# Selection rounds moved behind the value chunks, modulation sums spread, in a two-block fp32 kernel

## What is computed

```python
mod = (c_act @ w_ada[l] + b_ada[l])[:, None, :]
sh1, sc1, g1, sh2, sc2, g2 = jnp.split(mod, 6, axis=-1)
h = _rmsnorm(x, norm_g[l, 0]) * (1.0 + sc1) + sh1
y = _hybrid_mixer(h, ...)            # z = h @ w_in, mixers A, B, C, gates, w_out
x = x + g1 * _rmsnorm(y, norm_g[l, 1])

# mixer C, the sparse one: each query keeps 64 of up to 256 keys
score = jnp.einsum('bqh,bqhk->bqk', wb, jax.nn.relu(logits))
score = jnp.where(adm[None], score, NEG)
_, sel = lax.top_k(score, topk)      # topk = 64
...                                   # softmax over the selected keys only
# mixer B: s = q.k * scale + cum[q] - cum[k], cum = cumsum(log_sigmoid(f))
```

## Time and profile before

| | before |
|---|---|
| median of three runs | 850.33 us |
| the profiled execution | 851.06 us |
| its span, first to last instruction | 849.3 us |
| TensorE (PE) busy | 784.4 us, 92% |
| VectorE (DVE) busy | 531.4 us, 63% |
| ScalarE (ACT) busy | 405.7 us, 48% |
| DMA | 139.63 MB, mean 164 GB/s |
| mean granted TensorE clock | 0.970 |

### The profile page before, as it was taken

One profiled execution on the slowest core, in us unless ns is written; L12 is line 12 of the kernel. 1 busy time (PEld: TensorE's weight loads), 2 busy tenths in 40 slices (PEclk: granted clock), 3 DMA queues, 4 the chain that ended last, 5 costly groups with the idle time before them and its releaser, 6 DMA issues.

```text
span 849.3 us, 14466 instructions
## 1 busy us (share of the span) xinstructions
PE 784.4 (92%) x6114; PEld 748.9 (88%) x6114; DVE 531.4 (63%) x780; ACT 405.7 (48%) x541; POOL 68.8 (8%) x56
## 2 busy tenths in 40 slices
PE   2599999999899899999999999998989999998795
PEld 2499887888798799999999989998979999998694
DVE  4965978676564577777755457636556456656533
ACT  4363535454334554454434437437355545555514
POOL 0010000000130200000000110000025122212000
PEclk9699999999999999999999999899999999999999
DMA  9954356657424055554565434512516543341001
GB/s 358 401 206 161 130 199 237 259 213 274 158 100 149 19 201 188 191 198 162 212 236 212 176 137 165 198 51 100 186 50 205 196 156 143 103 145 51 1 2 49
DMA packets 20952, 139.63 MB, mean 164 GB/s; under 512 B 2356, under 2 KB 2996, under 8 KB 5016
## 3 DMA queue, kind: packets, MB, share of 16 engines
q1 hardware_dynamic: 20600, 137.80, 44.8%
q0 software_dynamic: 288, 0.92, 0.3%
HBM read 137.66 MB, written 1.05 MB: 163 GB/s over the span
## 4 chain that ended last, share of the span: by engine, by line
PE 68%; DVE 13%; ACT 7%; issue 7%; POOL 2%; DMA 2%; POOLq 0%; SPq 0%; ACTq 0%; DVEq 0%
PE res L1308 20%; PE res L1309 19%; PE res L1310 19%; PE pX L1392 3%; POOL sq L461 2%; ACT whi L537 2%; DVE wlo L858 2%; DVE dsc L1272 1%; PE pS L1410 1%; PE pX L1614 1%; DVE gates L871 1%; DVE hlo L885 1%; ACT sq L552 1%; PE pT L1431 1%; DVE y L1078 1%
## 5 line engine op out<-in xcount | busy, mean ns | idle before, releaser
L1308 PE MATMUL res<-hhi,whi 128*128 128x256 f32 x1160 | 337.1, 291 | 8.3 <-DVE hlo L885 6.6
L858 DVE TENSOR_TENSOR wlo<-raw,whi 128x2048 fp32r<-128x2048 f32 (+1 forms) x106 | 238.2, 2248 | 157.4 <-ACT whi L537 155.8
L1309 PE MATMUL res<-hhi,wlo 128*128 128x256 f32 x1160 | 330.6, 285 | 0.0
L1310 PE MATMUL res<-hlo,whi 128*128 128x256 f32 x1160 | 330.2, 285 | 0.0
L537 ACT ACTIVATE whi<-raw 128x2048 fp32r<-128x2048 f32 (+1 forms) x106 | 197.9, 1868 | 181.6 <-issue 138.2
L1308 PEld LDWEIGHTS res<-hhi,whi 128*128 128x128 f32 x1160 | 223.9, 193 | 16.2 <-issue 9.0
L1309 PEld LDWEIGHTS res<-hhi,wlo 128*128 128x128 f32 x1160 | 224.1, 193 | 0.2
L1310 PEld LDWEIGHTS res<-hlo,whi 128*128 128x128 f32 x1160 | 223.8, 193 | 0.2
L1308 PE MATMUL res<-uhi,whi 128*128 128x256 f32 x176 | 49.9, 283 | 0.0
L461 POOL TENSOR_TENSOR sq<-sq,rope 128x512 f32<-128x512 f32 x18 | 36.0, 2000 | 170.9 <-ACT sq L552 170.9
L1310 PE MATMUL res<-ulo,whi 128*128 128x256 f32 x176 | 49.3, 280 | 0.0
(11 more groups left out here) (253 smaller groups left out, 1158.7 us busy)
## 6 DMA issues: line engine op xcount, KB each, us to landing
raw<-in_wts SPq DMA_DIRECT2D x100, 1024.0 KB, 4.9
raw<-in_w_ada SPq DMA_DIRECT2D x16, 1024.0 KB, 4.8
gates<-in_w_ada SPq DMA_DIRECT2D x6, 1024.0 KB, 8.2
raw<-in_wts SPq DMA_DIRECT2D x4, 768.0 KB, 7.3
y<-in_w_ada SPq DMA_DIRECT2D x2, 1024.0 KB, 10.6
x<-in_xT SPq DMA_DIRECT2D x2, 512.0 KB, 6.0
outT<-x SPq DMA_DIRECT2D x4, 256.0 KB, 2.0
biasA<-in_relb SPq DMA_DIRECT2D x1, 768.0 KB
```

What stands on the lines that cost most here:

```text
L858: nc.vector.tensor_tensor(wlo[c % SPL][:, 0:b], raw[RAW_OF["w", c] % RAW][:, 0:b], whi[c % SPL][:, 0:b].bitcast(f32), ALU.subtract).then_i ...
L1308: mm(out, ah, bh, start=first, stop=False)
L1309: mm(out, al, bh, start=False, stop=False)
L1310: return mm(out, ah, bl, start=False, stop=last)
```

## The change

Two things. The modulation pieces 8 to 19 are placed behind other chunks of the stream (KK, QA, KB, VB, ZG, ZG + 1, ZG + 3, ZG + 6, ZG + 9, ZG + 10, ZG + 11, BRANCH), and with that are summed in the iterations of QC, KK, VA, QB, KB, VB, ZG + 1, ZG + 4, ZG + 7, ZG + 8, ZG + 9 and ZG + 10. The sixteen selection rounds run two per iteration from VB (ZG - 1) to ZG + 6, t = 0 first, behind the iteration's modulation sum. A semaphore that nobody waited for goes.

```diff
-ADA_AFTER = {ZG + i: 8 + i for i in range(12)} | {DOWN + 3 * i: 20 + i for i in range(4)}
+ADA_AFTER = {c: 8 + i for i, c in enumerate((KK, QA, KB, VB, ZG, ZG + 1, ZG + 3, ZG + 6, ZG + 9, ZG + 10, ZG + 11, BRANCH))}
+ADA_AFTER |= {DOWN + 3 * i: 20 + i for i in range(4)}
...
-        topk_done = sem("topk_done")
...
                 if b == KA:
...
-                    for i in range(8):
-                        topk_round(0, i)
                 if b == QB:
...
-                    for i in range(4):
-                        topk_round(1, i)
...
                 if b + 2 in ADA_AFTER:
                     ada(ADA_AFTER[b + 2])
-                if b in (ZG, ZG + 1):
-                    for i in range(4 + 2 * (b - ZG), 6 + 2 * (b - ZG)):
-                        topk_round(1, i)
-                    if b == ZG + 1:
-                        nc.vector.engine_nop().then_inc(topk_done, 1)
+                if ZG - 1 <= b < ZG + 7:
+                    t, i = (b - ZG + 1) // 4, 2 * ((b - ZG + 1) % 4)
+                    topk_round(t, i)
+                    topk_round(t, i + 1)
```

## The result

The changed kernel takes 854.27 us (median of 9 executions, 851.64 to 855.49); the kernel before, timed again beside it, 851.85 us (9 executions, 850.32 to 852.28). The ratio is 1.0029, 95% interval 1.0016 to 1.0041: it is slower by 2.5 us. I had forecast 851.6 us, no measurable change, with a range up to 853.3. The time lies outside the range, and the direction is not the one that I held likeliest. Timed a second time, on another occasion, the ratio was 1.0033 (1.0020 to 1.0045).

What follows compares the result with a forecast made beforehand. TensorE, busy 92% of the span, was taken as the bound. The terms 1.9 − 0.35 + 0.7 − 1.1 + 0.15 gave +1.3 us on the 850.33 us median, so 851.6 us, range 847.6 to 853.3.

Steps and rivals of the forecast that it cites:

- Clock, -0.35: Behind the wait before the first unit: clock falls as before, 0.7 us of the fall lies inside the wait, saving 0.35 us.
- The main mechanism: Load w12 queues behind a13, which needs a11's buffer; landing at 107.8 us, it delays low 12 and the bias behind it.
- The earlier loads, 0: Chunks before ZG: sums and loads placed earlier cost TensorE nothing; the 0.41 us wait at 98 us stays.
- ZG wait, +1.9: TensorE's wait before the first unit grows from 1.51 to 3.4 us because w12 lands late: +1.9 us.
- ZG + 1, +0.7: One chunk after ZG: a13's sum and two rounds delay low 13 and the normalised unit behind it: +0.7 us.
- ZG + 2, -1.1: Two chunks after ZG: w14 goes first of its pair, so the 1.08 us wait at 132.96 goes: -1.1 us.
- ZG + 3 on, 0 and +0.15: ZG + 3 to ZG + 9 cost nothing; a19's sum before low 24 lengthens the 1.03 us wait by 0.15 us.
- rival B: Slower: VectorE packed too tightly in ZG + 1 and ZG + 4, two more waits, +2.7 us, 853.0 us; chance 0.18.
- Rival A: The gain arrives: w12 is there when ScalarE asks, the clock stands, -2.6 us, 847.7 us; chance 0.24.

Runs made afterwards that it cites:

- after_again: The changed kernel unchanged, timed a second time against the kernel before: ratio 1.0033, times from 852.71 to 855.12 us.
- rounds_at_zg: The changed kernel with the selection rounds one chunk later, in ZG to ZG + 7: ratio 1.0027 to the kernel before.
- rounds_only: The kernel before with only the selection rounds moved as in the change, modulation sums as before: ratio 0.9989 (0.9976 to 1.0001).
- fill13: The changed kernel with 13 matmuls that nobody reads ahead of the first unit's wait for its bias: ratio 1.2 us below that of the changed kernel.
- before_bias_first: The kernel before with only the two biases of VB put ahead of low 12: ratio 0.9997 to the kernel before.
- w12_first: The changed kernel with two neighbouring loads exchanged, weight load w12 issued before modulation piece a13: ratio 0.9986 to the kernel before.
- a13_later: The changed kernel with modulation piece a13 loaded behind ZG + 2 instead of ZG + 1 and summed in ZG instead of VB: 848.98 us, ratio 0.9975.

## Why the prediction was wrong

The steps that failed are two on the clock's side of the sum and the level that it was put on. The term "Clock, -0.35 us" brought nothing, and the stretch from BRANCH to WOUT, which stood at nothing, took +0.51 us; the median of before was 851.85 us, not 850.33. The main mechanism, w12 late through the queue, was right.

Against the overlay from 98 us to WOUT, step by step:

- **The earlier loads, 0**: right. TensorE has no wait from 46 to 97 us, and the 0.4 us at 98 stays.
- **ZG wait, +1.9**: right in place, cause and size, +1.88. Load times, order of the queue, the bias behind low 12 and the drain behind high 12 are each shown by a run.
- **Clock, -0.35**: 0 in this pair, wrong by 0.35. The low stretch began and ended 0.4 us earlier in this execution (111.7 to 115.1 against 112.1 to 115.5), and TensorE resumed at 111.8, not 112.7: none of it fell into the wait. I had taken a place on the time axis from one execution, though each has its own. Over many executions the clock seems to cost more still: the mean granted clock of the eight executions in after_again's ratio is 0.9670, that of the 32 of before beside them 0.9687. A mean lower by 0.0017 is 0.0034 of the time more at the low level, some 3 us, and at 1.5 us for 3.4 that is a rough estimate of 1.3 us of the loss. Where they lie no profile shows; the 6.8 us behind the same wait in rounds_at_zg are a candidate.
- **ZG + 1, +0.7**: +0.90. ScalarE's copy released it (`upT`, L648), which follows the exponential behind the late low 13; not VectorE's normalised unit.
- **ZG + 2, -1.1**: -1.18, right. **ZG + 3 on, 0 and +0.15**: +0.18, right; rival B, waits in every full gate chunk, did not come.
- **BRANCH to WOUT, not in my sum**: +0.51. In before the clock is low from 238.4 to 241.8 us, in the matmuls on `ident` that only fill the time ahead of WOUT, and these last until 242.36, when the first low parts of the input are there. In after it had been low from 224.4 to 227.8, the filling matmuls end sooner, and TensorE waits 0.96 us for `hlo` (L1059). Half a microsecond of what the clock took in after before BRANCH was not given back here.

The filling matmuls and the start of WOUT, TensorE's timeline of before, then of after:

```profile
239.59 3.00 PE L1354 MATMUL pS<-ident 128*128 128x128 f32 x16
242.36 0.36 PE L1308 MATMUL res<-hhi,whi 128*128 128x256 f32 x1
...
240.61 1.95 PE L1349 MATMUL pS<-ident 128*128 128x128 f32 x16
```

This goes with where the clock is low in an execution, not with the change. Of the twelve traces, four (before, rounds_only, rounds_at_zg, fill13) have a low stretch that begins between 237 and 241 us, and none of them has this wait; the other eight have 0.94 to 0.96 us of it, before_bias_first too, which has the sums and rounds of before.

Together 2.25 instead of 1.3 us. So of the 2.25 us that I set beside the ratio's 2.5 some 0.5 belong to this pair of executions, and that the two agree so closely is partly luck.

The second half of the miss is the level. I put the sum on 850.33 us, the median of three executions of which two were at 850.3; with six more it is 851.85. The profiled one at 851.06 was no guide either. On the level of 851.85 the same sum gives 853.2, and the same range ends at 854.8, above the 854.27 measured: 1.5 of the 2.7 us by which the forecast missed are the level, the rest is the effect. The bound of the range above took in rival B, a mechanism, but not that executions of this kernel differ by 4 us with the clock, which three shown times could hide.

Rival A, the gain, came to nothing in the change and was right in kind as soon as one load moved: w12_first and a13_later are what it described, with -1.2 and -2.1 us by their ratios where it had -2.6. The Trainium skill (DMA: Bandwidth & Descriptors, Anatomy of one DMA) says that a wait for a semaphore is made by the issuing engine before dispatch; the rows of w12 agree: its own buffer was free from 94.5 us (low 10, started at 92.27), and it was issued at 99.96, behind a13's wait. The estimate from that page and from its Where 436 GB/s comes from, 7.9 us for a pair of loads, was too long: 6.89 and 6.97 us here. The page gives its fixed 2.0 us for loads that GpSimd issues, and these are SP's.

## What to carry to other kernels

When a load is moved in a shared queue with few buffers, write down for each load behind it whose buffer it waits for and what stands in front of it: here a load was late only because a neighbour waited for a buffer freed by VectorE, and exchanging the two was worth 0.4%. Put work that releases the bottleneck ahead of work that waits for a load, but look for the next late load first, since the same edit gave nothing in one kernel and 0.5% in another. And where a kernel's times step with the clock, take the level from many executions, lay two traces over each other by instruction, and compare stretches that hold the same clock.

## What I had not expected of the hardware

Executions of the kernel before spread over 847.95 to 852.81 us in one comparison, the shortest at a mean granted clock of 0.973 and most of the longest at 0.966, and one low stretch of 3.4 us costs 1.5 us. Low stretches come at different times in executions of unchanged code (40.4 us in before, none there in after), also where nothing was edited, and behind a wait of 3.4 us one lasted 3.4 us and another 6.8 us. A wait of 1.51 us was followed by a low stretch, ones of 1.39 and 1.06 us were not. Of two 1 MB loads issued 0.4 us apart, the first is usable 4.9 us and the second 6.9 us after its issue, but not always: w13 of before_bias_first took 8.2 us, and its last sixteenth came 1.2 us behind the others. Eleven of the twelve traces have loads before 300 us with such a late part, 0.8 us or more behind, at different places.
